# Attention units on VectorE: the order of norm, rotation, heads and low halves

## Chip, cores and metric

One core of a Trainium2 chip. The metric is the device time of one launch in microseconds, as the median of several runs. Beside it stands one execution recorded by the profiler, whose span is the time from its first to its last instruction.

## What is computed

One layer of a hybrid diffusion backbone on 256 latent tokens and 256 context tokens of width 2048, in float32. A modulated RMS norm and one input projection feed three mixers (attention, a gated linear recurrence, a short gated convolution), whose outputs go through gated projections, and then a product-key expert network follows. The change lies in attention: 16 query heads of width 128 in 4 groups of key and value heads, with a norm and a 2-D rotation of queries and keys, over 512 keys (256 context, 256 latent).

```python
ql = apply_rope(rmsnorm(qx.reshape(b_, t_, N_HEADS, HEAD_DIM), q_gain), cos, sin)
...
s = jnp.einsum('bqhgd,bkhd->bhgqk', q, k) * (HEAD_DIM ** -0.5)
p = jax.nn.softmax(s, axis=-1)
return jnp.einsum('bhgqk,bkhd->bqhgd', p, v)
```

## The kernel before

The five engines have their own instruction queues, written out in one function each, and every dependence between them is a semaphore that is waited for by a count. Nothing plans the order: the order in which a queue's Python code issues is the order in which the engine executes.

**Weights.** All large weights come as one stream of 1 MB halves through a ring of four slots (SyncE issues). Half a slot is a *piece* of 128 x 1024. To multiply float32 weights in TensorE's faster format, each piece is taken apart: ScalarE copies it rounded to `wh` (function `split`, line 973), VectorE subtracts that from the weights and stores the rest to `wl` (function `low`, line 1328), and TensorE makes three products of each (`wide`, lines 511 to 513: high by high, low by high, high by low). There are four `wh` and four `wl` buffers, so `split` of piece p waits until TensorE has used piece p−4.

**Attention** is cut into 32 *units* (`UNITS`), one for each head and tile of 128 queries, eight to a group. The four query projections, 8 pieces each, and the 8 pieces of the first gate run between them: `AT_UNIT` says which piece unit n takes; units 0 to 18, and then 20, 22, 24, 26, 28, 30, 32 and 33 have one, units 19, 21, 23 and so on have none. In unit n each engine issues, in this order:

- TensorE (from line 715): `score(n)` (line 686), which needs the exponential of n−2; the unit's piece; in some units `turned_queries` (line 676); `turned_weights(n-2)` (line 694), four transposes of stored weights into bank 6, which need the weights of n−2 scaled and the bank copied out; in even units `values(n/2-2)` (line 703), a head's product with the values, which needs the halves of the head before stored.
- ScalarE (from line 1155): the exponential of unit n with its row sum (line 1160), `split` of the piece four further on, then, where a rotation is due, the squares, root or stored queries, and last the copy `pT` of the turned weights of n−2 (line 1176).
- VectorE (from line 1705): the row maximum (line 1711) and the bias (line 1714) of unit n; `low` of the piece four further on, which waits for `split`; the norm of n−1, that is reciprocal (line 1721) and scaling of the weights in place (line 1723); in odd units from 5 on the high and low halves of a head (lines 1727 and 1729), which need its product; then the rotation's steps.

**Rotation of a group's queries.** `ROPE_AT` starts it for groups 1 to 3 in units 3, 11 and 19, five units before the group's first score; call that unit R. In unit R ScalarE squares both tiles of the group (`q_squares`, line 1131) and VectorE multiplies both by the cosines and sums the squares (`rope_cos`, lines 1673 and 1677). In unit R+1 ScalarE takes the root (`q_roots`, line 1136) and VectorE does four products with the sines and two sums (`rope_sin`, lines 1630 and 1687). In unit R+2 VectorE scales (`q_scale`, lines 1692 and 1694). TensorE turns the two tiles in units R+3 and R+4, and ScalarE stores them there (`store_queries`, line 1141). The squares lie in `qB`, which the sines' products overwrite, so these wait for the sums. VectorE's and ScalarE's steps of the rotation count on one semaphore (`Steps`), whose list of names has to follow the order of issue.

Behind attention, the second half of the output turn multiplies the finished heads (`out_turn`, `wide` on `br`); its first product needs the low half of head 15. From there on VectorE also forms the products of the modulation rows (line 1567), whose loads GpSimd issues once attention has left their buffers.

Of the kernel before, what the change touches and what calls it, by code (L numbers as in the profile page):

```python
# [24 lines left out]
ALU = mybir.AluOpType  # L25
# [3 lines left out]
P = 128  # L29
# [8 lines left out]
HEADS, KVH, HD = 16, 4, 128  # L38
# [19 lines left out]
KV0 = OUT0 + 4 * NCH  # L58
# [23 lines left out]
QPIECE0 = 2 * KPIECES  # L82
GPIECE0 = QPIECE0 + 8 * KVH
UNITS = 2 * HEADS
AT_UNIT = {n: QPIECE0 + 13 + n for n in range(19)}
AT_UNIT.update({n: GPIECE0 + i for i, n in enumerate((20, 22, 24, 26, 28, 30, 32, 33))})
ROPE_AT = {8 * g - 5: g for g in range(1, KVH)}
# [23 lines left out]
def build(nc, a_stream, a_params, a_consts, a_x, a_ctx, a_gates, a_gains, a_crow, a_wmod, a_bmod, a_gffn, a_keys, a_u, a_v, out):  # L111
    ctx = ExitStack()
    with ctx:
# [3 lines left out]
        def sem(name):  # L117
            return ctx.enter_context(nc.semaphore(name))
# [40 lines left out]
        cosq = con[:, P:P + T].rearrange("p (t d) -> p t d", t=2)  # L159
        sinq = con[:, P + T:P + 2 * T].rearrange("p (t d) -> p t d", t=2)  # L160
# [57 lines left out]
        qA = sb("qA", o, [P, 2, 4 * HD]); o += 4096  # L218
        qB = sb("qB", o, [P, 2, 4 * HD]); o += 4096
# [63 lines left out]
        ps = ctx.enter_context(nc.psum_tensor("ps", [P, 8, 2 * T], F32))  # L283
# [3 lines left out]
        piece_used = sem("piece_used")  # L287
# [51 lines left out]
        VK = Steps(sem("dve_keys"), ["ck", "sk0", "sk1", "cq", "sq0", "sq1", "ss", "rc", "n0", "g0", "n1", "g1"]  # L339
                   + [f"{w}{i}" for i in (2, 3) for w in ("n", "c", "s0", "s1", "a")])  # L340
        q_squared, q_rooted, q_turned, q_stored = (sem(f"q_{w}") for w in ("squared", "rooted", "turned", "stored"))
        VN = Steps(sem("dve_rope"), ["c0", "c1", "ss", "s00", "s01", "s10", "s11", "a0", "a1", "rc", "sc"])
        scored, p_turned, heads_done = sem("scored"), sem("p_turned"), sem("heads_done")
        exps_done, p_stored = sem("exps_done"), sem("p_stored")
        VQ = Steps(sem("dve_peaks"), ["mx", "nm"])
# [566 lines left out]
        def _(act):  # L912
# [212 lines left out]
            def q_squares(g):  # L1125

                act.wait_ge(piece_used, 2 * KV0 + QPIECE0 + 8 * (g + 1))
                if g:
                    act.wait_ge(q_turned, 2 * g)
                for t in (0, 1):  # L1130
                    fn(qB[:, t, :], ps[:, 2 * (g % 2) + t, :], ACT.Square).then_inc(q_squared, 1)

            def q_roots(g):

                act.wait_ge(*VN.at(g, "ss"))
                fn(qri[:, g % 2, :], qss[:, :], ACT.Sqrt, scale=1.0 / HD, bias=tiny[:, 1:2]).then_inc(q_rooted, 1)

            def store_queries(g, t):

                act.wait_ge(q_turned, 2 * g + t + 1)  # L1140
                fn(qT_[:, g % 2, :, t * P:(t + 1) * P], ps[:, 2 * (g % 2) + t, :].rearrange("p (h t) -> p h t", h=4), ACT.Copy).then_inc(q_stored, 1)
# [11 lines left out]
            for n in range(UNITS + 3):  # L1153
                if n < UNITS:
                    g, u = divmod(n, 8)
                    hh, qt = divmod(u, 2)
                    act.wait_ge(*VQ.at(n, "nm"))
                    if n >= 3:
                        act.wait_ge(p_turned, n - 2)
                    fn(pr[:, n % 3, :], ps[:, 4 + n % 2, :], ACT.Exp, scale=qri[:, g % 2, 4 * qt + hh:4 * qt + hh + 1],  # L1160
                       bias=bias_[:, n % 4:n % 4 + 1], accum_out=psum_[:, n % 4:n % 4 + 1]).then_inc(exps_done, 1)
                if n in AT_UNIT:
                    split(KV0, 0, 0, AT_UNIT[n] + 4)
                if n in ROPE_AT:
                    q_squares(ROPE_AT[n])
                if n - 1 in ROPE_AT:
                    q_roots(ROPE_AT[n - 1])
                for back in (3, 4):
                    if n - back in ROPE_AT:
                        store_queries(ROPE_AT[n - back], back - 3)  # L1170
                if 2 <= n < UNITS + 2:
                    m = n - 2
                    act.wait_ge(p_turned, m + 1)
                    if m >= 4:
                        act.wait_ge(heads_done, m // 2 - 1)
                    fn(pT[:, m // 2 % 2, :, m % 2 * P:(m % 2 + 1) * P], ps[:, 6, :].rearrange("p (k t) -> p k t", k=4), ACT.Copy)\
                        .then_inc(p_stored, 1)

            out_turn(1, OUT1, 0, ahead=12)
            with act.Fori(1, NW) as j:  # L1180
# [131 lines left out]
        def _(dve):  # L1312
# [11 lines left out]
            def low(first, turn, per, p):  # L1324

                s, q = (p // 2) % RING, p % 2
                dve.wait_ge(hi_done, turn * per + (2 * (first - LRU0) + p + 1))
                tt(wl[p % SPLITS][:, :, :], W[s][:, q * PIECE:(q + 1) * PIECE, :], wh[p % SPLITS][:, :, :].bitcast(F32), ALU.subtract)\  # L1328
                    .then_inc(lo_done, 1)
# [294 lines left out]
            heads4 = lambda x: x.rearrange("p (h d) -> p h d", h=4)  # L1624
            swaps = lambda x: x.rearrange("p (h a s j) -> p h a s j", h=4, a=2, s=2)

            def rotated(to, x, sin, s):

                s_ = sin.rearrange("p (a s j) -> p a s j", a=2, s=2)[:, :, s, :].unsqueeze(1).to_broadcast([P, 4, 2, HD // 4])
                return tt(swaps(to)[:, :, :, s, :], swaps(x)[:, :, :, 1 - s, :], s_, ALU.mult)  # L1630
# [32 lines left out]
            for p in range(17, 28):  # L1663
                low(KV0, 0, 0, p)

            def rope_cos(g):

                dve.wait_ge(piece_used, 2 * KV0 + QPIECE0 + 8 * (g + 1))
                if g:
                    dve.wait_ge(q_turned, 2 * g)  # L1670
                for t in (0, 1):
                    dve.wait_ge(q_squared, 2 * g + t + 1)
                    tt(heads4(qA[:, t, :]), heads4(ps[:, 2 * (g % 2) + t, :]), cosq[:, t:t + 1, :].to_broadcast([P, 4, HD]), ALU.mult)\
                        .then_inc(*VN.inc(f"c{t}"))
                if g:
                    dve.wait_ge(q_rooted, g)
                nc.vector.reduce_sum(qss[:, :], qB[:, :, :].rearrange("p t (h d) -> p (t h) d", h=4), AX.X).then_inc(*VN.inc("ss"))

            def rope_sin(g):

                dve.wait_ge(*VN.at(g, "ss"))
                for t in (0, 1):
                    for s in (0, 1):
                        rotated(qB[:, t, :], ps[:, 2 * (g % 2) + t, :], sinq[:, t, :], s).then_inc(*VN.inc(f"s{t}{s}"))
                for t in (0, 1):
                    dve.wait_ge(*VN.at(g, f"s{t}1"))
                    tt(qA[:, t, :], qA[:, t, :], qB[:, t, :], ALU.add).then_inc(*VN.inc(f"a{t}"))

            def q_scale(g):

                dve.wait_ge(q_rooted, g + 1)
                nc.vector.reciprocal(qri[:, g % 2, :], qri[:, g % 2, :]).then_inc(*VN.inc("rc"))
                dve.wait_ge(*VN.at(g, "rc"))
                tsc(qri[:, g % 2, :], qri[:, g % 2, :], SCALE, None, ALU.mult).then_inc(*VN.inc("sc"))

            rope_cos(0)
            low(KV0, 0, 0, 28)
            rope_sin(0)
            low(KV0, 0, 0, 29)
            q_scale(0)  # L1700
            low(KV0, 0, 0, 30)
# [3 lines left out]
            for n in range(UNITS + 4):  # L1705
                if n < UNITS:
                    g, u = divmod(n, 8)
                    hh, qt = divmod(u, 2)
                    at = slice(n % 4, n % 4 + 1)
                    dve.wait_ge(scored, n + 1)  # L1710
                    nc.vector.reduce_max(peak[:, at], ps[:, 4 + n % 2, :], AX.X).then_inc(*VQ.inc("mx"))
                    dve.wait_ge(*VQ.at(n, "mx"))
                    dve.wait_ge(*VN.at(g, "sc"))
                    tsc(bias_[:, at], peak[:, at], qri[:, g % 2, 4 * qt + hh:4 * qt + hh + 1], -1.0, ALU.mult, ALU.mult).then_inc(*VQ.inc("nm"))
                if n in AT_UNIT:
                    low(KV0, 0, 0, AT_UNIT[n] + 4)
                if 1 <= n < UNITS + 1:
                    m = n - 1
                    at = slice(m % 4, m % 4 + 1)
                    dve.wait_ge(exps_done, m + 1)  # L1720
                    nc.vector.reciprocal(pinv[:, at], psum_[:, at]).then_inc(*VP.inc("rs"))
                    dve.wait_ge(*VP.at(m, "rs"))
                    tsc(pr[:, m % 3, :], pr[:, m % 3, :], pinv[:, at], None, ALU.mult).then_inc(*VP.inc("pn"))
                if n >= 5 and n % 2:
                    hd = (n - 5) // 2
                    dve.wait_ge(heads_done, hd + 1)
                    nc.vector.tensor_copy(br[0][:, hd, :], ps[:, 7, 0:T]).then_inc(*VH_.inc("hi"))
                    dve.wait_ge(*VH_.at(hd, "hi"))
                    tt(br[1][:, hd, :], ps[:, 7, 0:T], br[0][:, hd, :].bitcast(F32), ALU.subtract).then_inc(*VH_.inc("lo"))  # L1729
                if n in ROPE_AT:  # L1730
                    rope_cos(ROPE_AT[n])
                if n - 1 in ROPE_AT:
                    rope_sin(ROPE_AT[n - 1])
                if n - 2 in ROPE_AT:
                    q_scale(ROPE_AT[n - 2])

            dve.wait_ge(*VY.at(0, "s"))
            out_turn(1, OUT1, 0, range(4), ahead=12)
# [388 lines left out]
```

## Time and profile before

| | |
|---|---|
| median of 3 runs | 2977.57 us (2971.10 to 2978.94) |
| profiled execution | 2972.38 us, span 2970.3 us |
| TensorE, matrix products | 2621.7 us busy, 88% |
| VectorE | 1947.6 us busy, 66% |
| ScalarE | 976.3 us busy, 33% |
| mean granted TensorE clock | 0.976 of full speed |
| attention's units | about 757 to 926 us |

The profile lists instructions of every engine with their start and length and infers who released an instruction that the engine had sat idle for. Matrix products are pipelined: a record of 0.39 us may be followed by the next one 0.23 us after its start. The granted clock is given in parts of full speed, 2.4 GHz.

### The profile page before, as it was taken

To read this page: it belongs to the slowest core of one execution; us is meant where nothing else is said; L and a number is where in the kernel's file an instruction comes from. 1 tells how busy PE (TensorE), PEld (TensorE's weight loads), DVE (VectorE), ACT (ScalarE), POOL (GpSimd) and SP (SyncE) were. 2 spreads that over 40 slices of the span, in tenths; PEclk is the share of its full clock that TensorE was granted. 3 is DMA by queue.
4 is the path that set the end of the run, shared out by engine and by line. 5 is a ranking of instruction groups with operands and counts; after the bars stand their busy time and mean duration, and the time that the engine had idled before them with its cause. 6 is when DMAs were issued, how large, how long until landed. Compare 5 with 4: busy or idle time off the path is not lost.

```text
span 2970.3 us, 31536 instructions
## 1 busy us (share of the span) xinstructions
PE 2621.7 (88%) x11037; PEld 1778.8 (60%) x11037; DVE 1947.6 (66%) x2649; ACT 976.3 (33%) x1333; POOL 568.4 (19%) x580
## 2 busy tenths in 40 slices
PE   7999998999989999999999987777878777777777
PEld 3588876888767899998887843333424323333322
DVE  4689997444666788887555766665555665666656
ACT  5578775433554433333444211111011111111100
POOL 0000000000000000000000463333343333433333
PEclk9999999999999999999999999999999999999999
DMA  8733335543325888887566899999999999999998
GB/s 347 276 116 118 113 113 185 188 153 116 126 86 217 334 320 333 324 336 278 206 252 245 338 414 421 421 421 422 421 414 421 421 422 421 395 421 422 421 422 342
DMA packets 126514, 902.93 MB, mean 304 GB/s; under 512 B 14016, under 2 KB 15552, under 8 KB 17216
## 3 DMA queue, kind: packets, MB, share of 16 engines
q0 software_dynamic: 82944, 604.02, 49.3%
q1 hardware_dynamic: 38448, 276.84, 25.1%
q10 hardware_dynamic: 5008, 20.66, 1.8%
q8 instruction: 58, 0.95, 0.1%
q14 instruction: 56, 0.46, 0.0%
HBM read 899.33 MB, written 2.13 MB: 303 GB/s over the span
## 4 chain that ended last, share of the span: by engine, by line
PE 50%; DMA 35%; issue 7%; DVE 6%; ACT 2%; POOL 1%; POOLq 0%; DVEq 0%; SPq 0%; ACTq 0%
DMA u<-in_peer_u,idx 31%; PE ps L468 12%; PE ps L511 8%; PE ps L513 8%; PE ps L512 8%; PE ps L483 6%; PE ps L852 2%; DMA v<-in_peer_v,idx 2%; PE ps L591 2%; DVE u L1922 1%; DMA w<-in_stream 1%; DVE wl L1328 1%; PE ps L525 1%; PE ps L703 1%; ACT wh L973 1%
## 5 line engine op out<-in xcount | busy, mean ns | idle before, releaser
L875 PE MATMUL ps<-v,dg 128*128 128x512 f32 x1920 | 893.0, 616 | 277.4 <-DMA v<-in_peer_v,idx 165.1
L1922 DVE SCALAR_TENSOR_TENSOR u<-u,hN 128x2048 f32<-128x2048 f32 x256 | 586.6, 2292 | 473.5 <-DMA u<-in_peer_u,idx 462.2
L875 PEld LDWEIGHTS ps<-v,dg 128*128 128x128 f32 x1920 | 362.6, 196 | 802.5 <-issue 521.8
L1328 DVE TENSOR_TENSOR wl<-w,wh 128x1024 fp32r<-128x1024 f32 x432 | 524.8, 1223 | 382.6 <-ACT wh L973 382.1
L973 ACT ACTIVATE wh<-w 128x1024 fp32r<-128x1024 f32 x432 | 455.3, 1059 | 612.8 <-PE ps L513 410.6
L2016 POOL DMA_INDIRECT u<-in_peer_u,idx x256 | 268.4, 1049 | 940.3 <-DVE u L1922 551.3
L468 PE MATMUL ps<-both,wh 128*128 128x256 f32 x2048 | 371.8, 284 | 0.0
L1276 ACT ACTIVATE dg<-con,wt 128x128 f32<-128x128 f32 x240 | 92.7, 399 | 802.3 <-PE ps L875 797.3
L468 PEld LDWEIGHTS ps<-both,wh 128*128 128x128 f32 x2048 | 320.1, 192 | 3.5 <-issue 3.3
L468 PE MATMUL ps<-both,wl 128*128 128x256 f32 x1024 | 289.8, 283 | 0.0
L2005 POOL DMA_DIRECT2D mr<-in_wmod x64 | 34.0, 532 | 1336.3 <-DVE br_lo L1729 925.3
L2026 POOL DMA_INDIRECT v<-in_peer_v,idx x256 | 265.8, 1038 | 99.2 <-issue 85.0
L511 PE MATMUL ps<-wh,both 128*128 128x512 f32 x640 | 263.1, 411 | 8.9 <-DVE wl L1328 8.9
L513 PE MATMUL ps<-wh,both 128*128 128x512 f32 x640 | 251.0, 392 | 0.0
L512 PE MATMUL ps<-wl,both 128*128 128x512 f32 x640 | 250.6, 392 | 0.0
L468 PEld LDWEIGHTS ps<-both,wl 128*128 128x128 f32 x1024 | 196.6, 192 | 0.0
L483 PE MATMUL ps<-both,wh 128*128 128x512 f32 x512 | 160.9, 395 | 0.9 <-DVE wl L1328 0.9
L511 PE MATMUL ps<-wh,br_hi 128*128 128x512 f32 x384 | 150.2, 391 | 2.4 <-DVE wl L1328 1.2
L512 PE MATMUL ps<-wl,br_hi 128*128 128x512 f32 x384 | 149.4, 389 | 0.0
L513 PE MATMUL ps<-wh,br_lo 128*128 128x512 f32 x384 | 149.4, 389 | 0.0
L1567 DVE SCALAR_TENSOR_TENSOR mr<-mr,srow 128x2048 f32<-128x2048 f32 x64 | 146.3, 2287 | 0.7 <-DMA mr<-in_wmod 0.7
L511 PEld LDWEIGHTS ps<-wh,both 128*128 128x128 f32 x640 | 121.1, 189 | 41.2 <-DVE wl L1328 11.0
(267 smaller groups left out, 2868.9 us busy)
## 6 DMA issues: line engine op xcount, KB each, us to landing
w<-in_stream SPq DMA_DIRECT2D x258, 1024.0 KB, 4.9
mr<-in_wmod POOLq DMA_DIRECT2D x64, 1024.0 KB, 6.8
wg<-in_gates ACTq DMA_DIRECT2D x8, 512.0 KB, 3.3
wx<-in_stream SPq DMA_DIRECT2D x4, 1024.0 KB, 8.0
u<-in_peer_u,idx POOLq DMA_INDIRECT x256, 16.7
v<-in_peer_v,idx POOLq DMA_INDIRECT x256, 18.0
xs<-in_ctx ACTq DMA_DIRECT2D x1, 2048.0 KB, 8.8
xs<-in_x ACTq DMA_DIRECT2D x1, 2048.0 KB, 17.0
```

Source lines behind the costliest of these rows:

```text
L468: last = mm(ps[:, bank, c0:c0 + T], w[:, kk, cols], src[part_][:, k, :], start=(k == 0 and bank not in started), stop=(k == KT - 1), skip_ ...
L483: last = mm(ps[:, banks + blk, :].rearrange("p (s t) -> p s t", s=2), w[:, kk, cols], both[:, :, part_, k, :], start=(k == 0 and n == 0), ...
L511: mm(ps[:, bank + i, :], of[0][:, k, rows], hi[:, kk, :], start=(k == 0), stop=False)
L512: mm(ps[:, bank + i, :], of[0][:, k, rows], lo[:, kk, :], start=False, stop=False)
L513: last = mm(ps[:, bank + i, :], of[1][:, k, rows], hi[:, kk, :], start=False, stop=(k == KT - 1))
L875: last = mm(ps[:, b, :], dg[:, k % 4, :], V[n % NV][:, b * 512:(b + 1) * 512], start=(k == 0), stop=(k == TOPK - 1))
L973: fn(wh[p % SPLITS][:, :, :], W[s][:, q * PIECE:(q + 1) * PIECE, :], ACT.Copy).then_inc(hi_done, 1)
L1328: tt(wl[p % SPLITS][:, :, :], W[s][:, q * PIECE:(q + 1) * PIECE, :], wh[p % SPLITS][:, :, :].bitcast(F32), ALU.subtract)\
L1567: stt(mr[n % NM][:, :], mr[n % NM][:, :], 1.0, srow[:, :], ALU.mult, ALU.mult, accum_out=mcols[:, n:n + 1])\
L1922: stt(U[n % NU][:, :], U[n % NU][:, :], 1.0, hN[:, t, :], ALU.mult, ALU.mult, accum_out=dot[:, t, k:k + 1])\
L2016: nc.gpsimd.indirect_dma_start(out=U[n % NU][:, :], out_offset=None, in_=a_u, in_offset=bass.IndirectOffsetOnAxis(ap=idx[:, odd, t, k:k + ...
L2026: nc.gpsimd.indirect_dma_start(out=V[n % NV][:, :], out_offset=None, in_=a_v, in_offset=bass.IndirectOffsetOnAxis(ap=idx[:, odd, t, k:k + ...
```

## The change

Three orders of issue change, and no instruction is added or removed. On ScalarE, the copy of turned weights moves in front of squares, root and stored queries, and the root comes in unit R+2 instead of R+1. On VectorE, norm and a head's halves move in front of the low half. The rotation is spread by tile: first tile's cosine in R behind the low half; second tile's cosine in R+1 behind the norm, and the sums at that unit's end; first tile's sines and sum in R+2, second tile's in R+3, both behind the norm; the scale at the end of R+3.

```diff
@@ semaphore steps
-        VN = Steps(sem("dve_rope"), ["c0", "c1", "ss", "s00", "s01", "s10", "s11", "a0", "a1", "rc", "sc"])
+        VN = Steps(sem("dve_rope"), ["c0", "c1", "ss", "s00", "s01", "a0", "s10", "s11", "a1", "rc", "sc"])
@@ ScalarE, unit n
                 if n in AT_UNIT:
                     split(KV0, 0, 0, AT_UNIT[n] + 4)
-                if n in ROPE_AT:
-                    q_squares(ROPE_AT[n])
-                if n - 1 in ROPE_AT:
-                    q_roots(ROPE_AT[n - 1])
-                for back in (3, 4):
-                    if n - back in ROPE_AT:
-                        store_queries(ROPE_AT[n - back], back - 3)
                 if 2 <= n < UNITS + 2:
...
+                if n in ROPE_AT:
+                    q_squares(ROPE_AT[n])
+                if n - 2 in ROPE_AT:
+                    q_roots(ROPE_AT[n - 2])
+                for back in (3, 4):
+                    if n - back in ROPE_AT:
+                        store_queries(ROPE_AT[n - back], back - 3)
@@ VectorE, the steps
-            def rope_cos(g):
+            def rope_cos(g, t):
...
+            def q_sums(g):
...
-            def rope_sin(g):
+            def rope_sin(g, t):
 
                 dve.wait_ge(*VN.at(g, "ss"))
-                for t in (0, 1):
-                    for s in (0, 1):
-                        rotated(qB[:, t, :], ps[:, 2 * (g % 2) + t, :], sinq[:, t, :], s).then_inc(*VN.inc(f"s{t}{s}"))
-                for t in (0, 1):
-                    dve.wait_ge(*VN.at(g, f"s{t}1"))
-                    tt(qA[:, t, :], qA[:, t, :], qB[:, t, :], ALU.add).then_inc(*VN.inc(f"a{t}"))
+                for s in (0, 1):
+                    rotated(qB[:, t, :], ps[:, 2 * (g % 2) + t, :], sinq[:, t, :], s).then_inc(*VN.inc(f"s{t}{s}"))
+                dve.wait_ge(*VN.at(g, f"s{t}1"))
+                tt(qA[:, t, :], qA[:, t, :], qB[:, t, :], ALU.add).then_inc(*VN.inc(f"a{t}"))
@@ VectorE, unit n
-                if n in AT_UNIT:
-                    low(KV0, 0, 0, AT_UNIT[n] + 4)
                 if 1 <= n < UNITS + 1:
...
+                if n - 1 in ROPE_AT:
+                    rope_cos(ROPE_AT[n - 1], 1)
+                for back in (2, 3):
+                    if n - back in ROPE_AT:
+                        rope_sin(ROPE_AT[n - back], back - 2)
                 if n >= 5 and n % 2:
...
+                if n in AT_UNIT:
+                    low(KV0, 0, 0, AT_UNIT[n] + 4)
                 if n in ROPE_AT:
-                    rope_cos(ROPE_AT[n])
+                    rope_cos(ROPE_AT[n], 0)
                 if n - 1 in ROPE_AT:
-                    rope_sin(ROPE_AT[n - 1])
-                if n - 2 in ROPE_AT:
-                    q_scale(ROPE_AT[n - 2])
+                    q_sums(ROPE_AT[n - 1])
+                if n - 3 in ROPE_AT:
+                    q_scale(ROPE_AT[n - 3])
```

Group 0 is rotated ahead of the units as before, tile by tile.

## Rows read from the trace of the kernel before

**Rows 1.** Busy time by stretch: us, each engine's busy us (instructions), TensorE clock, DMA share, GB/s.

```profile
757.00:926.00 169.00, 153.01 (x675) 113.65 (x674) 106.63 (x222) 88.73 (x148) 0.28 (x1) 0.99 0.26 94
872.00:878.00 6.00, 6.00 (x22) 4.36 (x23) 5.32 (x15) 2.94 (x5) 0.00 (x0) 0.72 0.00 0
926.00:1100.00 174.00, 172.70 (x840) 145.79 (x839) 131.46 (x115) 69.05 (x66) 13.14 (x25) 1.00 0.82 322
```

**Rows 2.** Waits between 757 and 926 us: total us, times, longest.

```profile
ACT pr L1160 <- DVE bias L1714: 70.2, 32, 4.4
...
PE ps L694 <- DVE pr L1723: 6.3, 5, 2.1
...
PE ps L694 <- ACT pT L1176: 5.1, 3, 2.4
...
PE ps L703 <- DVE br_lo L1729: 3.4, 3, 2.9
```

**Rows 3.** Timeline of TensorE: start, us, engine, line, op, tiles, count [idle before <-releaser].

```profile
792.10 0.66 PE L694 MATMUL ps<-con,pr 128*128 128x128 f32 x4 [2.06 <-DVE pr L1723]
...
805.06 1.02 PE L686 MATMUL ps<-kT,qT__125 128*128 128x512 f32 x2
...
813.16 1.89 PE L703 MATMUL ps<-pT,vT 128*128 128x256 f32 x8
814.89 1.02 PE L686 MATMUL ps<-kT,qT__125 128*128 128x512 f32 x2
...
887.79 1.02 PE L686 MATMUL ps<-kT,qT__125 128*128 128x512 f32 x2
888.85 0.65 PE L694 MATMUL ps<-con,pr 128*128 128x128 f32 x4
...
895.11 1.02 PE L686 MATMUL ps<-kT,qT__125 128*128 128x512 f32 x2
...
922.52 1.96 PE L703 MATMUL ps<-pT,vT 128*128 128x256 f32 x8 [2.92 <-DVE br_lo L1729]
925.46 0.50 PE L511 MATMUL ps<-wh,br_hi 128*128 128x512 f32 x1 [0.98 <-DVE br_lo L1729]
```

**Rows 4.** Timeline of VectorE, one plain unit with a head in front of it.

```profile
802.16 0.42 DVE L1727 CAST br_hi<-ps 128x256 fp32r<-128x256 f32 x1
...
802.96 0.68 DVE L1711 TENSOR_REDUCE peak<-ps 128x1 f32<-128x512 f32 x1
803.67 0.21 DVE L1714 TENSOR_SCALAR bias<-peak,qri 128x1 f32<-128x1 f32 x1
805.77 1.23 DVE L1328 TENSOR_TENSOR wl<-w,wh 128x1024 fp32r<-128x1024 f32 x1 [1.88 <-ACT wh L973]
806.91 0.16 DVE L1721 RECIPROCAL pinv<-psum 128x1 f32<-128x1 f32 x1
...
807.50 0.68 DVE L1711 TENSOR_REDUCE peak<-ps 128x1 f32<-128x512 f32 x1
```

**Rows 5.** Timeline of ScalarE: a table load, a plain unit, the last copy.

```profile
785.21 1.28 ACT L1160 ACT_TABLE_LOAD   x1
...
803.92 0.78 ACT L1160 ACTIVATE pr<-ps,bias,qri 128x512 f32<-128x512 f32 x1 [2.55 <-DVE bias L1714]
...
804.69 1.04 ACT L973 ACTIVATE wh<-w 128x1024 fp32r<-128x1024 f32 x1
...
920.23 0.58 ACT L1176 ACTIVATE pT<-ps 128x512 f32<-128x512 f32 x1
```

**Rows 6.** Timeline of VectorE, the rotation of group 1.

```profile
777.99 1.28 DVE L1673 TENSOR_TENSOR qA<-ps,con 128x512 f32<-128x512 f32 x2
779.19 1.21 DVE L1677 TENSOR_REDUCE qss<-qB 128x8 f32<-128x1024 f32 x1
...
784.87 1.41 DVE L1630 TENSOR_TENSOR qB<-ps,con 128x256 f32<-128x256 f32 x4
786.19 1.29 DVE L1687 TENSOR_TENSOR qA<-qA,qB 128x512 f32<-128x512 f32 x2
```

More of the change, by code:

```diff
@@ L1664, in _ @@
                 low(KV0, 0, 0, p)
-            def rope_cos(g):
-                dve.wait_ge(piece_used, 2 * KV0 + QPIECE0 + 8 * (g + 1))
-                if g:
-                    dve.wait_ge(q_turned, 2 * g)
-                for t in (0, 1):
-                    dve.wait_ge(q_squared, 2 * g + t + 1)
-                    tt(heads4(qA[:, t, :]), heads4(ps[:, 2 * (g % 2) + t, :]), cosq[:, t:t + 1, :].to_broadcast([P, 4, HD]), ALU.mult)\
-                        .then_inc(*VN.inc(f"c{t}"))
+            def rope_cos(g, t):
+                if t == 0:
+                    dve.wait_ge(piece_used, 2 * KV0 + QPIECE0 + 8 * (g + 1))
+                    if g:
+                        dve.wait_ge(q_turned, 2 * g)
+                dve.wait_ge(q_squared, 2 * g + t + 1)
+                tt(heads4(qA[:, t, :]), heads4(ps[:, 2 * (g % 2) + t, :]), cosq[:, t:t + 1, :].to_broadcast([P, 4, HD]), ALU.mult)\
+                    .then_inc(*VN.inc(f"c{t}"))
+            def q_sums(g):
                 if g:
@@ L1677, in rope_cos @@
                 nc.vector.reduce_sum(qss[:, :], qB[:, :, :].rearrange("p t (h d) -> p (t h) d", h=4), AX.X).then_inc(*VN.inc("ss"))
-            def rope_sin(g):
+            def rope_sin(g, t):
                 dve.wait_ge(*VN.at(g, "ss"))
-                for t in (0, 1):
-                    for s in (0, 1):
-                        rotated(qB[:, t, :], ps[:, 2 * (g % 2) + t, :], sinq[:, t, :], s).then_inc(*VN.inc(f"s{t}{s}"))
-                for t in (0, 1):
-                    dve.wait_ge(*VN.at(g, f"s{t}1"))
-                    tt(qA[:, t, :], qA[:, t, :], qB[:, t, :], ALU.add).then_inc(*VN.inc(f"a{t}"))
+                for s in (0, 1):
+                    rotated(qB[:, t, :], ps[:, 2 * (g % 2) + t, :], sinq[:, t, :], s).then_inc(*VN.inc(f"s{t}{s}"))
+                dve.wait_ge(*VN.at(g, f"s{t}1"))
+                tt(qA[:, t, :], qA[:, t, :], qB[:, t, :], ALU.add).then_inc(*VN.inc(f"a{t}"))
             def q_scale(g):
@@ L1694, in q_scale @@
                 tsc(qri[:, g % 2, :], qri[:, g % 2, :], SCALE, None, ALU.mult).then_inc(*VN.inc("sc"))
-            rope_cos(0)
+            rope_cos(0, 0)
+            rope_cos(0, 1)
+            q_sums(0)
             low(KV0, 0, 0, 28)
-            rope_sin(0)
+            rope_sin(0, 0)
+            rope_sin(0, 1)
             low(KV0, 0, 0, 29)
```

## Prediction

> **What bounds the kernel now.** The span is 2970.3 us, the profiled execution 2972.38, so 2.1 lie around the span; the median of the runs is 2977.57, 5.2 above that execution. I take the change in us off the median. The edits touch one stage, attention's 32 units, between 757 and 926 us, so I read that stage: first the busy times of stretches [rows 1]. TensorE works 153.01 of 169 us there, VectorE 106.63, ScalarE 88.73, and in the stage behind it TensorE works 172.70 of 174. TensorE is the bound; the stage can give back its idle 16.0 us and little more.
>
> Then the waits of that stretch [rows 2]: TensorE waits 6.3 us for scaled weights (L1723), 5.1 for a copy of turned weights on ScalarE and 3.4 for a head's low half, 2.92 of that being the last head [rows 3]; another 0.98 comes when the next stage begins. Behind these stands a ring: ScalarE waits 70.2 us for the bias, and VectorE in turn sits in front of each low half until ScalarE has rounded the piece. That idling is no loss in itself, but VectorE has other work in that time.
>
> The ring in a plain unit [rows 4, 5]: maximum at 802.96, bias at 803.67, exponential 0.25 later, rounding 0.77 later at 804.69, low half 1.08 later at 805.77, norm 1.14 later at 806.91, next maximum 0.59 after that. From the bias' end, 803.88, VectorE idles 1.89 us. That makes 4.54 us, and 5.34 with a head's halves (0.80, 802.16 to 802.96), so 9.88 for two units. TensorE needs 9.83 for two (scores at 805.06 and 814.89, without a gap) [rows 3]. The two are level, so VectorE has no reserve. The rotation of a group (L1673, L1677, L1630, L1687: 1.28 + 1.21 + 1.41 + 1.29 as records, some 4.8 by starts) [rows 6] comes in two lumps of 2.3 and 2.5 us, on the ring, and TensorE stands still after each: 2.06 us before 792.10 for instance [rows 3].
>
> **Part 1, norm and heads in front of the low half.** Nothing is added or removed: the reciprocal and scaling of n−1 (0.59) and the head's halves (0.80) go into the time in which VectorE waits for the rounding. The window from the bias' end to the low half is 0.25 + 0.77 + 1.08 − 0.21 = 1.89 us; 0.59 + 0.80 = 1.39 fits. The ring shrinks to 0.71 + 0.25 + 0.77 + 1.08 + 1.14 = 3.95 us a unit against TensorE's 4.92. What these instructions wait for is there: the exponential of n−1 ran before the rounding of n−1, and a head's product ends before the score that the maximum already waited for. Behind the low half stands only the next maximum, and TensorE takes that piece four pieces later. TensorE now sets the plain units, with 0.97 us in reserve in each. A plain unit gets no shorter: 9.83 for two remains.
>
> **Part 2, the rotation in halves.** By unit after the start unit R (3, 11, 19) VectorE gets: R, the first cosine behind the low half, +0.60; R+1, the second cosine under the wait (0.59 + 0.60 < 1.89, no head there) and the sums behind the low half, +1.1; R+2, the first half's sines and sum, 0.66 + 0.60 + about 0.12 for the wait on the sines now right in front of the sum, so with norm and head 2.77, 0.88 over the window; R+3, norm and second half, 1.97, 0.08 over, then the scale, +0.3. That is 3.0 us over four units with 3.9 in reserve: no wait of TensorE in groups 1 and 2. The halves are wanted in R+3 and R+4, where TensorE turns them behind its piece; each is ready about one piece early (2.7 us: 9.83, less the 7.32 of two units with one piece between 887.79 and 895.11, with 0.2 for a small wait in these) [rows 3]. I price these two groups at nothing; the cover is that reserve.
>
> In group 3, units 19, 21 and 23 have no piece. Two units take TensorE 7.32 us, and VectorE 3.95 + 0.71 + 0.21 + 0.59 + 0.80 = 6.3, a reserve of 1.0 in two units, while the first half's 1.38 in unit 21 has no low half to hide under. Two such pairs hold 2.0 against 0.6 + 1.1 + 1.4 added: about **1.1 us** of waits in units 22 and 23 is new. Bounds: 0, and 4.8, a whole rotation.
>
> **Part 3, ScalarE.** The copy of turned weights (record 0.58) goes in front of squares, root and stored queries, so the bank for the next transposes is free before them: 5.1 us of waits go. Squares (about 1 us) now end 1.1 after the copy; VectorE's cosine waits for them, but has the 1.14 us low half first. The root with its table comes a unit later; root and return to the exponential take a table load of 1.28 each [rows 5], about 2.9 with the root itself, beside some 2.6 of other work in a unit of over 4.9. The Trainium skill, page ScalarE: Activation LUTs, Rules for kernel authors, budgets about 2.7 us for each switch; the rows here say 1.28 and decide. By the page ScalarE would end 2.8 later in each group, which only group 3 would feel: 2963.9.
>
> **Part 4, the last head.** The last head's product at 922.52 waited for the halves of the head before, which stood behind the last low half. These now go first, and the gate becomes the last copy of turned weights, start 920.23 [rows 5] + 0.58 and a tenth for the hand-off = 920.9: 1.6 saved, 1.5 of wait left. The 0.98 behind it stays.
>
> **Clock.** From 872 to 878 us the granted clock averages 0.72, falling from 2.4 to 1.2 GHz right behind the longest of these waits (2.4 us) [rows 1, 2]: 6 × 0.28 = 1.7 us, which goes with the wait. The Trainium skill (TensorE: Matmul & The Clock Gate, Part 1) says that activity keeps the clock up and that the place of a drop varies from run to run. The trace has one drop behind eight waits on scaled weights and copies, which fits; by the page the 1.7 may be missing from the median, which gives 2962.8.
>
> **Sum.** Ten waits of 6.3 + 5.1 + 0.5 (two short ones for a head) = 11.9. Each costs 0.16 more than its idle, since a record ends 0.16 after the point where the next one would start (813.16 + 1.89 against 814.89) [rows 3]: 1.6. Clock 1.7. Four small ones near the end, like 888.85, which is 1.06 behind its scores (record 1.02, so 0.86 without a wait): 0.8. Last head 1.6. New: −1.1. Gain 11.9 + 1.6 + 1.7 + 0.8 + 1.6 − 1.1 = **16.5 us**; 2977.57 − 16.5 = **2961.1** (2955.9 for an execution like the profiled one). No stage reaches across the seam but the weight ring, and DMA share is 0.26 here, so what follows moves up whole.
>
> **Rivals.**
> 1. *The halves come too tight.* If hand-offs in a rotation run some tenths over, TensorE waits 0.75 for each of six halves: 4.5 back, 2965.6. For: they are now made one unit ahead, not two. Against: 2.7 us of lead. 0.13.
> 2. *ScalarE stays the holder.* The 5.1 + 0.5 and the clock's 1.7 stay: gain 9.2, 2968.4. For: root and two tables still lie in one unit. Against: the copy is in front of them. 0.08.
> 3. *Given back behind.* The next stage starts earlier and its loads (DMA share 0.82) bind: 0 to 4 left, about 2975.5. For: that share. Against: TensorE is 99% busy there, and the modulation rows load only after attention's end, so they shift with it. 0.09.
> 4. *Slower.* VectorE falls a full unit behind in every rotation, because first cosine and sums sit in front of the next maximum, and TensorE waits for both halves in units R+3 and R+4. Slower by over 8.9 needs 25.4 us of new waits, 4.2 for each of six halves; at a full unit of 4.9 the total is 29.4, minus 16.5: 2990.5. Against: the rotation adds 3.0 us where 3.9 are free. 0.04.
>
> That the new order isn't what runs can be left out: the order of a queue is the order of issue.
>
> **Numbers.** Forecast 0.66, spread ±3 by the runs of before (2971.1 to 2978.94) and by the bounds of group 3 and clock: 2956 to 2966. To take in rivals 1 and 2 the range goes up to 2971, and down to 2954 (whole idle, all 20 us with the overhangs, and scatter). About 0.3%, 8.9 us, can be told from nothing. Faster: forecast 0.66, rival 1 most of 0.13, a part of 2: 0.80. Same: 0.15. Slower: 0.05.
>
> **What would show it.** The seam to the next stage, now at 925.46, comes at about 909; TensorE idle there under 4 us; no wait for scaled weights in units 5, 6, 13 and 14; ScalarE's wait for the bias smaller; low halves starting behind norm; no clock under 0.9 at group 3; the last head's product with 1.5 of idle in place of 2.92; the stretch behind as long as before. It is wrong if TensorE waits at L676 by more than 1 us, or if the stage shrinks and the end doesn't.

## The result and the profile after

The changed kernel takes 2954.35 us (median of 4 runs, 2952.29 to 2957.18) against 2977.32 for the kernel before (4 runs); the ratio is 0.9926, 95% interval 0.9915 to 0.9938, that is 22 us less (18.5 to 25.3). The profiled executions are 2955.63 and 2972.38 us, 16.75 apart. A later comparison of the same two (below) gives 0.9938 (0.9925 to 0.9951), 18.5 us. The forecast was 16.5.

First the busy times of the stretches that answer to [rows 1], in the same columns (us, busy time of TensorE, its weight loads, VectorE, ScalarE and GpSimd, TensorE's clock, DMA share, GB/s):

```profile
757.00:909.00 152.00, 148.92 (x676) 113.33 (x675) 107.39 (x222) 89.61 (x148) 0.16 (x1) 1.00 0.29 102
872.00:878.00 6.00, 6.00 (x27) 4.37 (x26) 4.49 (x11) 3.15 (x8) 0.00 (x0) 1.00 0.03 11
909.00:1083.00 174.00, 173.24 (x844) 146.32 (x843) 131.84 (x115) 69.30 (x67) 13.27 (x25) 1.00 0.84 326
```

TensorE is idle for 3.1 of 152 us where it was idle for 16.0 of 169, and the clock is at its full level through the stage. In the 174 us behind it TensorE is as busy as before (173.24 and 172.70 us).

The waits of the stage (who waited for whom, total us, times, longest), against [rows 2]:

```profile
ACT pr L1160 <- DVE bias L1718: 50.7, 29, 2.8
...
PE ps L703 <- ACT pT L1169: 1.3, 1, 1.3
PE ps L511 <- DVE br_lo L1736: 1.0, 1, 1.0
...
PE ps L694 <- ACT pT L1169: 0.5, 1, 0.5
PE ps L676 <- DVE qA L1688: 0.4, 1, 0.4
```

The waits for scaled weights, 6.3 us before, are gone. What is left is what the forecast had listed: two short waits in group 3, the last head's, and the 0.98 at the seam, where the next stage begins. ScalarE waits 50.7 us for the bias in place of 70.2.

A plain unit on VectorE, against [rows 4]:

```profile
801.59 0.21 DVE L1718 TENSOR_SCALAR bias<-peak,qri 128x1 f32<-128x1 f32 x1
801.72 0.15 DVE L1723 RECIPROCAL pinv<-psum 128x1 f32<-128x1 f32 x1
801.91 0.49 DVE L1725 TENSOR_SCALAR pr<-pr,pinv 128x512 f32<-128x512 f32 x1
802.31 0.42 DVE L1734 CAST br_hi<-ps 128x256 fp32r<-128x256 f32 x1
802.76 0.42 DVE L1736 TENSOR_TENSOR br_lo<-ps,br_hi 128x256 fp32r<-128x256 f32 x1
804.75 1.23 DVE L1328 TENSOR_TENSOR wl<-w,wh 128x1024 fp32r<-128x1024 f32 x1 [1.57 <-ACT wh L973]
805.90 0.68 DVE L1715 TENSOR_REDUCE peak<-ps 128x1 f32<-128x512 f32 x1
```

The norm now starts 0.13 us behind the bias' start, and a head's halves follow it. The low half starts 3.16 us behind the bias' start, later than the 2.10 of before, because its rounding on ScalarE now waits for TensorE to have used the piece four earlier:

```profile
803.66 1.06 ACT L973 ACTIVATE wh<-w 128x1024 fp32r<-128x1024 f32 x1 [0.96 <-PE ps L513]
```

So TensorE sets the pace here, and the ring is slack.

TensorE, against [rows 3]:

```profile
799.80 1.02 PE L686 MATMUL ps<-kT,qT__125 128*128 128x512 f32 x2
...
809.60 1.02 PE L686 MATMUL ps<-kT,qT__125 128*128 128x512 f32 x2
...
862.48 0.66 PE L676 MATMUL ps<-con,qA 128*128 128x128 f32 x4 [0.39 <-DVE qA L1688]
...
867.20 0.63 PE L694 MATMUL ps<-con,pr 128*128 128x128 f32 x4 [0.45 <-ACT pT L1169]
...
905.61 1.99 PE L703 MATMUL ps<-pT,vT 128*128 128x256 f32 x8 [1.25 <-ACT pT L1169]
908.58 0.50 PE L511 MATMUL ps<-wh,br_hi 128*128 128x512 f32 x1 [0.98 <-DVE br_lo L1736]
```

Two plain units still take 9.80 us from score to score (799.80 to 809.60), 9.83 before. The stage's end, its first product on the finished heads, comes at 908.58 where it was 925.46 [rows 3]. Below, *attention's length* is measured from the first score to that product: 758.09 to 908.58, **150.49 us**; before, 757.87 (first score, in the timeline of TensorE) to 925.46, **167.59 us**. Behind it the changed kernel runs for 2044.82 us and the one before for 2044.84.

### The profile page after: what moved, and what is told of

The parts are those of the page before. It is cut to its first block, busy times and chain, and to the rows that moved or that the text cites. A ratio compares the mean times of both kernels' runs of the same rounds, so it can differ in the third digit from the quotient of the medians.

```text
span 2953.4 us, 31536 instructions
## 1 busy us (share of the span) xinstructions
PE 2619.9 (89%) x11037; PEld 1779.9 (60%) x11037; DVE 1948.0 (66%) x2649; ACT 977.1 (33%) x1333; POOL 572.6 (19%) x580
## 4 chain that ended last, share of the span: by engine, by line
PE 49%; DMA 36%; issue 7%; DVE 5%; ACT 1%; POOL 1%; POOLq 0%; DVEq 0%; SPq 0%; ACTq 0%
DMA u<-in_peer_u,idx 33%; PE ps L468 12%; PE ps L511 8%; PE ps L513 8%; PE ps L512 8%; PE ps L483 6%; DVE u L1931 2%; DMA v<-in_peer_v,idx 2%; PE ps L591 2%; DMA w<-in_stream 1%; PE ps L703 1%; PE ps L686 1%; PE ps L525 1%; DVE wl L1328 1%; POOL u L2025 1%
```

## The experiments

Each kernel is given by its edit. The numbers quoted for attention's length come from the timeline of TensorE in each profile, the ratios from runs of both kernels on one chip.

### Only the norm in front of the low half

```diff
 (kernel before, VectorE, unit n)
-                if n in AT_UNIT:
-                    low(KV0, 0, 0, AT_UNIT[n] + 4)
                 if 1 <= n < UNITS + 1:
...
+                if n in AT_UNIT:
+                    low(KV0, 0, 0, AT_UNIT[n] + 4)
                 if n >= 5 and n % 2:
```

> Only the norm goes in front of the low half; heads, rotation and ScalarE's order stay as before. Attention from its first score to the next stage's first product on the heads takes 167.6 us before and 150.5 after. Ring theory (the low half's wait in front of other work makes VectorE late, and the rotation's lumps only show that it has no reserve): 8 to 10 us shorter, 158 to 160. Lump theory (the rotation's two lumps hold TensorE and the spreading gives the gain): at most 3 shorter, since both lumps are still there.

Measured: attention 158.44 us, ratio 0.9967 (0.9954 to 0.9980), 9.8 us less than before. The reordering of two short instructions, with both lumps of the rotation left in place, gives about half of the whole gain. The lump theory, which allowed 3 us, falls. TensorE's waits (total us, times, longest):

```profile
PE ps L703 <- DVE br_lo L1729: 4.8, 3, 2.9
PE ps L694 <- ACT pT L1176: 4.6, 5, 2.8
```

No wait for scaled weights is left (6.3 us before), but those for the copy of turned weights stay almost whole (5.1 us before, [rows 2]).

### Norm and heads in front of the low half

```diff
 (kernel before, VectorE, unit n)
-                if n in AT_UNIT:
-                    low(KV0, 0, 0, AT_UNIT[n] + 4)
                 if 1 <= n < UNITS + 1:
...
                 if n >= 5 and n % 2:
...
+                if n in AT_UNIT:
+                    low(KV0, 0, 0, AT_UNIT[n] + 4)
```

> Norm and heads in front of the low half, rotation in its old two lumps, ScalarE's order old. Ring theory: 12.5 to 14.5 us shorter than before, 153 to 155, with waits of about 1 us per lump left and the last head's 1.6 gained. Lump theory: at most 5 shorter.

Measured: attention 153.66 us, ratio 0.9948 (0.9933 to 0.9963), 15.5 us less than before. TensorE's waits for ScalarE, the second of them in front of the last head's product (total us, times, longest):

```profile
PE ps L694 <- ACT pT L1176: 3.9, 4, 2.8
...
PE ps L703 <- ACT pT L1176: 1.3, 1, 1.3
```

What remains of the two lumps is 3.9 us of waits for the copy of turned weights, not about 1 us at each lump as expected but 2.75 of it at group 3. ScalarE in front of that copy, in unit R+1:

```profile
859.67 0.78 ACT L1160 ACTIVATE pr<-ps,bias,qri 128x512 f32<-128x512 f32 x1 [2.45 <-DVE bias L1714]
...
861.50 1.28 ACT L1136 ACT_TABLE_LOAD   x1
862.79 0.30 ACT L1136 ACTIVATE qri<-qss,tiny 128x8 f32<-128x8 f32 x1
863.00 0.58 ACT L1176 ACTIVATE pT<-ps 128x512 f32<-128x512 f32 x1
```

Two things make the copy late there: the exponential has waited 2.45 us for a bias that stands behind VectorE's cosines and sums, and the root with its table, 1.5 us, stands in front of the copy.

### Only the rotation in halves

```diff
 (changed kernel, VectorE, unit n; ScalarE's squares, root in R+2 and stored queries in front of the copy)
+                if n in AT_UNIT:
+                    low(KV0, 0, 0, AT_UNIT[n] + 4)
                 if 1 <= n < UNITS + 1:
...
-                if n in AT_UNIT:
-                    low(KV0, 0, 0, AT_UNIT[n] + 4)
```

> Only the rotation spread over four units (root in unit R+2); the low half stays in front of norm and heads, ScalarE's order old. Ring theory: nothing gained, -1 to +2 us against before, 167 to 169.5, with the waits moved from the scaled weights to the turned queries. Lump theory: most of the gain, 7 to 14 us shorter.

Measured: ratio 1.0009 (0.9999 to 1.0018). The spreading alone gains nothing. The profiled execution, the slowest of ten (2983.68 us; the others go down to 2972.08), has 174.51 us of attention, more than expected; here are its waits and its clock (waits as above; stretches with TensorE's clock in the last column but two):

```profile
PE ps L676 <- DVE qA L1688: 9.2, 4, 3.1
...
PE ps L694 <- DVE pr L1727: 2.2, 4, 1.3
PE ps L694 <- ACT pT L1176: 0.5, 1, 0.5
```

```profile
834.00:844.00 10.00, 7.77 (x25) 6.22 (x26) 7.84 (x20) 5.08 (x9) 0.00 (x0) 0.66 0.19 56
882.00:892.00 10.00, 8.34 (x29) 6.37 (x30) 4.87 (x14) 3.37 (x7) 0.00 (x0) 0.66 0.30 107
```

TensorE now waits up to 3.1 us for the turned queries, which the spreading has moved one to two units nearer to their use; in this execution the clock fell in four places, behind each of its waits of 2.75 to 3.11 us, and two of these falls took 10 × 0.34 = 3.4 us each. Turned queries that come late because VectorE is behind are what rivals 1 and 4 of the forecast feared; they arise with the old ring. The waits for the copy, though, are down from 5.1 us to 0.5, with ScalarE's copy still behind squares and root.

### The kernel before once more

No edit.

> The kernel before once more, unchanged. The medians of before and after are 23 us apart, the two profiled executions 16.8. If the rest is scatter between executions of before, the executions here spread over 2971 to 2979 again and the profile shows attention at 167.6 +- 3 with the rest of the time elsewhere. If executions of before usually have a longer attention (more falls of the clock, 1.7 us each) than the one profiled, this profile has a good chance to show 170 to 174 and clocks under 1 at more than one rotation.

Measured: 2975.42 us (11 runs, 2971.87 to 2980.20), ratio to the kernel before 0.9999 (0.9990 to 1.0009), attention 170.20 us, 2.6 more than in the execution on which the forecast rests. The waits and the clock (timeline of TensorE; then two stretches):

```profile
791.68 0.66 PE L694 MATMUL ps<-con,pr 128*128 128x128 f32 x4 [2.05 <-DVE pr L1723]
792.56 3.16 PE L703 MATMUL ps<-pT,vT 128*128 128x256 f32 x8 [0.23 <-DVE br_lo L1729]
...
882.18 0.65 PE L694 MATMUL ps<-con,pr 128*128 128x128 f32 x4 [1.11 <-DVE pr L1723]
...
923.20 3.49 PE L703 MATMUL ps<-pT,vT 128*128 128x256 f32 x8 [2.91 <-DVE br_lo L1729]
927.66 0.50 PE L511 MATMUL ps<-wh,br_hi 128*128 128x512 f32 x1 [0.97 <-DVE br_lo L1729]
```

```profile
792.00:798.00 6.00, 5.77 (x19) 4.03 (x17) 3.98 (x10) 2.79 (x5) 0.00 (x0) 0.72 0.06 8
922.00:928.00 6.00, 3.83 (x10) 2.82 (x10) 1.87 (x5) 1.81 (x2) 0.08 (x1) 0.72 0.49 175
```

The same program, in another execution. The clock fell behind the waits of 2.05 us at 791.68 and of 2.91 us at 923.20, and did not fall behind the wait at 872 us as it did in the other [rows 1]. A wait of 1.11 us stands at 882.18 that the execution first profiled does not have: there TensorE ran at half speed just before, and VectorE had caught up by then. Each fall takes 6 × 0.28 = 1.7 us, but a fall at group 3 hides a wait of 1.1 + 0.16 and so costs only some 0.4.

### Two more executions of the kernel before

No edit.

> A third look at the kernel before. Clock theory: attention's length is 165.9 us plus 1.7 for each fall of the clock, so 167.6, 169.3 or 171.0, by which of its waits the clock falls in.

> A fourth look at the kernel before, with the same expectation: 165.9 us plus 1.7 for each fall, and a set of falls that differs from the other looks.

Measured: 168.68 us with one fall (791 us), and 170.16 us with two (793 and 923 us). Both expectations miss the base: without falls it is about 167.0 and not 165.9, because only a fall at group 3 takes the 1.11 us wait away. The three executions without such a fall agree on it: 168.68 − 1.7; and with two falls, of which the one at the seam lies partly behind attention's end (4.33 and 4.46 us from the last head's product to the seam in place of 2.94), 170.16 − 1.7 − 1.4 and 170.20 − 1.7 − 1.5, all 167.0 to 167.1. The fourth execution was also expected to differ in its set of falls, and has that of the execution above. The four executions of the kernel before have a mean of 169.16 us; the one that I had predicted from, 167.59, is the shortest.

### The changed kernel once more

No edit.

> The changed kernel once more, unchanged. Clock theory (before, TensorE's waits of 2 us and more let the clock fall in one to several places per execution, each 1.7 us or more, and the changed kernel has no such waits): attention 150.5 +- 0.3 us again, no fall of the clock in it, and executions closer together than those of the kernel before. Scatter theory (the executions differ elsewhere, attention gives 16.5 and the rest of the difference of the medians is chance): the ratio to the kernel before comes out at 0.9945 with more rounds; clock theory: 0.993.

Measured: attention 150.44 us, no fall of the clock, ratio 0.9938 (0.9925 to 0.9951). The length and the absence of falls are as the clock theory has them. The ratio decides nothing: it lies between the two theories' 0.9930 and 0.9945, and its interval holds both. And the executions lie over 7.7 us (2954.48 to 2962.14), little closer together than the 10.4 of the kernel before on that chip, so that point is a miss. Some of this scatter lies ahead of attention: the first score came at 760.84 in place of 758.09.

### ScalarE's order back

```diff
 (changed kernel, ScalarE, unit n)
+                if n in ROPE_AT:
+                    q_squares(ROPE_AT[n])
...
                 if 2 <= n < UNITS + 2:
...
-                if n in ROPE_AT:
-                    q_squares(ROPE_AT[n])
...
```

> The changed kernel with ScalarE's order back: squares, root and stored queries in front of the copy of turned weights. Part 3 of the prediction took 5.1 us of waits as going with this order. Ring theory (the copy was late only because its unit's exponential and rounding were late): attention 150.5 to 151.5 us, nothing to be measured. Order theory (the copy waits behind squares and table): 154 to 156, with waits of about 1.5 us per group for the copy.

The root stays in unit R+2. Measured: attention 150.39 us, ratio 0.9941 (0.9927 to 0.9955). TensorE's waits for ScalarE:

```profile
PE ps L703 <- ACT pT L1176: 1.3, 1, 1.3
...
PE ps L694 <- ACT pT L1176: 0.9, 2, 0.5
```

With the rotation spread, ScalarE's new order is worth nothing: 0.9 us of waits for the copy where the changed kernel has 0.5, and the turned queries' 0.4 is gone in exchange. So the 5.1 us of waits for the copy in the kernel before [rows 2] did not need the new order to go. Nor do they go with norm and heads: 4.6 and 3.9 us were left there. They went in both kernels that have the rotation spread, the root in R+2 and ScalarE's old order: this one and the one with the old ring (0.5). Whether the earlier bias or the later root did it was not separated, and what the new order would bring with the rotation in lumps was not run.

### A head's halves behind the low half

```diff
 (changed kernel, VectorE, unit n)
+                if n in AT_UNIT:
+                    low(KV0, 0, 0, AT_UNIT[n] + 4)
                 if n >= 5 and n % 2:
...
-                if n in AT_UNIT:
-                    low(KV0, 0, 0, AT_UNIT[n] + 4)
```

> The changed kernel with a head's halves behind the low half again. Plain units have 0.97 us in reserve and the halves take 0.80, so ring theory: only the last head is late again, +1.6 us, attention 152 us. Rival (heads on the ring cost their 0.80 in each of 16 units): 160 or more.

Measured: attention 153.76 us, of which 1.7 is a fall of the clock at the last head's wait; ratio 0.9943 (0.9930 to 0.9956).

```profile
PE ps L703 <- DVE br_lo L1738: 2.9, 1, 2.9
```

Without the fall 152.1 us, as expected. Once the norm is in the window and the rotation is spread, the heads' 0.80 in a unit is free, and their place matters for the last one alone.

### The last unit's weights in front of the last piece

```diff
 (changed kernel, TensorE, unit n)
+                if n == UNITS + 1:
+                    turned_weights(n - 2)
                 if n in AT_UNIT:
...
-                if 2 <= n < UNITS + 2:
+                if 2 <= n < UNITS + 1:
                     turned_weights(n - 2)
 (ScalarE, unit n)
-                if n in AT_UNIT:
+                if n in AT_UNIT and n != UNITS + 1:
                     split(KV0, 0, 0, AT_UNIT[n] + 4)
                 if 2 <= n < UNITS + 2:
...
+                if n in AT_UNIT and n == UNITS + 1:
+                    split(KV0, 0, 0, AT_UNIT[n] + 4)
```

> The changed kernel, with the transposes of the last unit's weights and their copy in front of the last piece and its rounding instead of behind. The 1.25 us of wait before the last head's product should go: attention 149.1 us (-1.4). A rival: the last piece then ends later against the sigmoid and the wait reappears there, 150.5.

Measured: attention 149.47 us, ratio 0.9927 (0.9914 to 0.9939), median 2956.29 us against 2958.05 for the changed kernel on the same chip. TensorE at the end:

```profile
901.22 0.60 PE L694 MATMUL ps<-con,pr 128*128 128x128 f32 x4
...
904.43 1.89 PE L703 MATMUL ps<-pT,vT 128*128 128x256 f32 x8
907.85 0.50 PE L511 MATMUL ps<-wh,br_hi 128*128 128x512 f32 x1 [1.53 <-DVE br_lo L1740]
```

The wait of 1.25 us in front of the last head's product is gone: counted from the first score that product starts 1.5 us earlier. Some 0.5 came back behind it, where the seam's 0.98 has grown to 1.53. Attention is 1.0 us shorter; the times cannot tell it from nothing. Behind attention, TensorE waits here for the low half of a piece:

```profile
960.58 0.50 PE L511 MATMUL ps<-wh,br_hi 128*128 128x512 f32 x1 [3.03 <-DVE wl L1332]
```

In the two executions of the changed kernel that wait is 0.62 and 0.98 us, so this execution gives more back there than it gained.

### More work on VectorE, in both kernels

```diff
 (both kernels, VectorE, unit n)
                     dve.wait_ge(scored, n + 1)
+                    nc.vector.reduce_max(spare[:, n % 8:n % 8 + 1], ps[:, 4 + n % 2, :], AX.X)
```

> The changed kernel with one more maximum (0.69 us of VectorE, its result unused) in front of the maximum of each of the 32 units, 22 us of VectorE's time. Reserve theory (plain units have 0.97 us of reserve, a rotation and the units without a piece use it up): plain units hide all of it, rotations and the units from 19 on do not; attention 7 to 8 us longer, about 158. Rival (VectorE's order is still what TensorE waits for in plain units): 20 us or more longer.

> The kernel before with the same more work. Ring theory: VectorE's ring and TensorE's need are level there (9.88 against 9.83 us for two units), so nearly all of the 22 us shows: attention 18 to 21 us longer than before, 186 to 189, and more falls of the clock. Lump theory: plain units have room, 5 to 10 longer.

The result of the added maximum is not used. Measured in the changed kernel: attention 156.12 us, 5.7 more for 22 us of work, ratio to the kernel before 0.9946 (0.9929 to 0.9962). In the kernel before: 184.67 us, 15.5 over the mean of its four executions, ratio 1.0045 (1.0028 to 1.0062). The stretch of the changed kernel, and the waits of TensorE in the other (line numbers are one or two higher by the added lines):

```profile
757.00:918.00 161.00, 153.88 (x693) 115.46 (x692) 128.12 (x258) 90.06 (x151) 0.00 (x0) 1.00 0.28 100
```

```profile
PE ps L695 <- DVE pr L1725: 15.8, 15, 2.6
...
PE ps L695 <- ACT pT L1177: 5.9, 3, 2.1
```

The same work costs nearly three times as much in the old order. In the changed kernel VectorE is busy for 128.12 us of 161, against 107.39 of 152, and TensorE still works 153.88. Both came out below what was expected (7 to 8, and 18 to 21). Part of that is the size of the work, taken from records; by starts an added maximum takes 0.60 us, so 32 of them 19 us (VectorE, kernel before with the added maximum):

```profile
808.66 0.68 DVE L1712 TENSOR_REDUCE spare<-ps 128x1 f32<-128x512 f32 x1
809.26 0.68 DVE L1713 TENSOR_REDUCE peak<-ps 128x1 f32<-128x512 f32 x1
```

In the kernel before with this work the clock fell in three places (797, 875 and 885 us), so some of the 15.5 us is the clock's.

## Why the prediction was right, point by point

**The bound and the sign** were right. The gain lies in attention alone: the rest behind it agrees to 0.02 us in the two profiled executions (closer than such times repeat, see below), so rival 3 (given back behind) is excluded, and TensorE's idle there fell from 16.0 to 3.1 us, against "under 4".

**Part 1** was right, and it carries the change. In attention's length the norm is worth 10.7 us (169.16, the mean of before, to 158.44), the heads 4.8 more (153.66), rotation and ScalarE together 3.2 (150.45). Of the 10.7, 2.2 are the clock's falls (169.16 − 167.0), which that one execution did not have; since it keeps waits of up to 2.9 us, that may be chance. The reserve that the sum leant on is shown by the added work: the same maximum in each unit cost 15.5 us in the old order and 5.7 in the new.

**Part 2**, priced at nothing for groups 1 and 2 and at 1.1 us for group 3: no wait in the first two, and in group 3 the waits of 0.39 and 0.45 us at 862.48 and 867.20, with 0.16 each for the overhang 1.2 us. They are in units 22 and 23, where they were expected. Rival 1 did not come.

**Part 3** put 5.1 us of waits down to ScalarE's order, and this step failed: with that order back the length is the same (150.39). The sum was not hurt, since the waits do go, but by another edit than the one credited: 4.6 and 3.9 us of them stay when norm and heads are moved, and they go with the spread rotation and its later root, which the sum had as a cost only. That the total came out is partly luck. The releaser in a wait's row is the last link of a chain; the rows alone do not say which link to move.

**Part 4**: 1.6 us forecast. The wait for the last head fell from 2.92 to 1.25 us, 1.7, and putting the heads back costs 152.1 − 150.5 = 1.6.

**The clock and the size.** In the pair of executions that the sum was made for, attention is 167.59 − 150.49 = 17.1 us shorter, against 16.5. The medians are 22 us apart, and 2954.35 lies below the 2956 to 2966 given for the forecast itself; it is inside the whole range only because that went down to 2954. The step that was mis-sized is the one that took the clock's cost from one execution: "6 × 0.28 = 1.7 us, which goes with the wait", one fall. Three further executions of the kernel before have falls in other places, two of them have two, and with none at group 3 a wait of 1.1 us is there besides. Their mean is 169.7 us, 2.1 over the execution that I read. Against the mean of all four the stage has become 18.7 us shorter, within both intervals (18.5 to 25.3, and 14.6 to 22.3), and the forecast of 16.5 lies just outside the first. The Trainium skill (TensorE: Matmul & The Clock Gate, Part 1) says that the point where the clock changes level varies from run to run; it tells this of the rise under a first run of products, and the four executions show it of the falls. I had used it to ask whether the 1.7 might be missing, and never whether there could be more. What is left between 18.7 and the first comparison's 22 is not settled; it is within the scatter of start and end (the first score came between 756.3 and 760.8 us in all six executions of these two kernels, and the part behind attention took 2043.9 to 2049.8 us).

## What to carry to other kernels

When an engine in a ring of in-order queues is idle in front of one instruction and has other ready work behind it, put that work into the wait before anything else: here two instructions of together 0.6 us did more than spreading 5 us of rotation; the spreading alone did nothing, and on top of them 3 us. Read the reserve and not the busy share: two engines level at 9.88 and 9.83 us leave no room for any lump, and one extra instruction in each unit measures that room. And price a clock that falls behind waits from several executions, for one may have caught it at its best.

## What the runs showed of the hardware

In every execution of the kernel before the granted clock fell at least once in attention or at its seam, from 2.4 to 1.2 GHz, behind waits of 2.05 to 2.92 us, and not behind each such wait: behind the one before 873 us in one execution, 791 in another, 793 and 923 in two, and never behind the one of 2.05 to 2.08 us at 837. Each of these falls lost 1.7 us of TensorE's time. A fall can last longer: with the rotation spread in the old ring two lost 3.4 us each. The shortest wait with a fall behind it was 1.94 us (885 us, the kernel before with more work). In the five executions with no wait above 1.53 us in attention or at its seam (the changed kernel twice, ScalarE's order back, the last weights first, and the changed kernel with more work on VectorE) there was no fall there. Nor does a longer wait always bring a fall: with only the norm moved, waits of 2.77 and 2.91 us remained, with the heads moved too one of 2.75, and the clock held. I had not expected a slowed TensorE to help: at half speed it let VectorE catch up and so removed a wait of 1.1 us ten microseconds later.
